# Where the spare projection groups stand in the state-space stage: two whole groups per quarter instead of seven portions

## What is computed

```python
def mixer_block(hn, s_gla, s_c, s_n, s_m, s_re, s_im, P, l):
    (gq, gk, gv, gr, ga, mq, mk, mv, mo, mi, mf, su, za, zb, zc) = split_in(hn @ P['w_in'][l])
    ...
    y_c, re_new, im_new = s5_ssm(su.astype(f32), ...)

def s5_ssm(u, h0_re, h0_im, ...):
    ug = u.reshape(B, T, S5_GROUPS, S5_GROUP)
    bu_re = jnp.einsum('btgc,gpc->btgp', ug, bb_re)
    bu_im = jnp.einsum('btgc,gpc->btgp', ug, bb_im)
    ...
    _, _, hr, hi = lax.associative_scan(combine, (a_re, a_im, bu_re, bu_im), axis=1)
    y = (jnp.einsum('btgp,gcp->btgc', hr, c_re) - jnp.einsum('btgp,gcp->btgc', hi, c_im)
         + d.reshape(S5_GROUPS, S5_GROUP) * ug).reshape(B, T, S5_WIDTH)
    y = jax.nn.gelu(y)
    y = y * jax.nn.sigmoid(y @ w_glu)
```

## Time and profile before

| | |
|---|---|
| median of 3 runs | 2631.93 us |
| the profiled execution's own time | 2638.09 us |
| span of its profile | 2636.3 us |
| TensorE busy, share of the span | 2351.4 us, 89% |
| the state-space stage | from 166.60 to 345.70 |

### The profile page before, as it was taken

The page is one execution under the profiler, slowest core; times in us unless marked ns, Lnnn a source line. Parts: engine busy times, 40 slices in busy tenths (PEclk is TensorE's granted clock), DMA queues, the critical chain, the costliest instruction groups (busy, mean ns, idle before and its releaser), DMA issues.

```text
span 2636.3 us, 34651 instructions
## 1 busy us (share of the span) xinstructions
PE 2351.4 (89%) x14712; PEld 2249.5 (85%) x14712; DVE 1149.7 (44%) x1264; ACT 574.7 (22%) x716; POOL 268.0 (10%) x411
## 2 busy tenths in 40 slices
PE   5799977779985579999999999779999999999996
PEld 5699857568975469999999998669999999999995
DVE  4634413432236532122223432134665666666566
ACT  4422222221321122111212211232211111111112
POOL 6898300000000000000000000000000000000000
PEclk9899988878986669999999999989999999999997
DMA  6211113001210002121112124301111111111111
GB/s 226 87 50 49 49 67 104 17 34 34 80 40 5 16 5 77 48 80 48 47 42 104 48 72 161 135 9 48 52 47 49 48 49 41 49 49 48 41 49 68
DMA packets 35928, 156.35 MB, mean 59 GB/s; under 512 B 4176, under 2 KB 4240, under 8 KB 32336
## 3 DMA queue, kind: packets, MB, share of 16 engines
q1 hardware_dynamic: 27504, 100.22, 11.2%
q0 software_dynamic: 6864, 43.84, 4.3%
q10 hardware_dynamic: 1440, 10.49, 1.0%
HBM read 135.68 MB, written 19.02 MB: 59 GB/s over the span
## 4 chain that ended last, share of the span: by engine, by line
PE 81%; DVE 9%; ACT 5%; issue 3%; DMA 1%; POOL 1%; DVEq 0%; ACTq 0%; POOLq 0%
PE ps L249 21%; PE ps L250 21%; PE ps L252 21%; PE ps L1933 1%; DVE ATT L1565 1%; PE ps L989 1%; PE ps L359 1%; PE ps L360 1%; PE ps L362 1%; DVE CC L1228 1%; DMA scratch_yc<-YC 1%; ACT PA L2000 1%; PE ps L1308 1%; DVE GT L387 1%; PE ps L1609 1%
## 5 line engine op out<-in xcount | busy, mean ns | idle before, releaser
L249 PE MATMUL ps<-XH,WH 128*128 128x344 f32 x1608 | 520.7, 326 | 26.9 <-DVE WL L243 20.7
L250 PE MATMUL ps<-XL,WH 128*128 128x344 f32 x1464 | 469.7, 324 | 0.0
L249 PE MATMUL ps<-XN,WH 128*128 128x344 f32 x1248 | 396.6, 321 | 4.3 <-issue 4.1
L243 DVE TENSOR_TENSOR WL<-WRAW,WH 128x1024 fp32r<-128x1024 f32 x175 | 224.5, 1283 | 393.0 <-ACT WH L238 392.0
L250 PE MATMUL ps<-XN,WH 128*128 128x344 f32 x1248 | 394.7, 319 | 0.0
L252 PE MATMUL ps<-XH,WL 128*128 128x344 f32 x1608 | 345.0, 323 | 0.0
L249 PEld LDWEIGHTS ps<-XH,WH 128*128 128x128 f32 x1608 | 308.3, 192 | 30.9 <-issue 27.6
L238 ACT ACTIVATE WH<-WRAW 128x1024 fp32r<-128x1024 f32 x175 | 184.3, 1054 | 561.0 <-PE ps L252 545.0
L250 PEld LDWEIGHTS ps<-XL,WH 128*128 128x128 f32 x1464 | 280.7, 192 | 0.1
L252 PEld LDWEIGHTS ps<-XH,WL 128*128 128x128 f32 x1608 | 273.0, 191 | 0.0
L252 PE MATMUL ps<-XN,WL 128*128 128x344 f32 x1248 | 262.9, 319 | 0.0
(11 more groups left out here) (503 smaller groups left out, 3293.2 us busy)
## 6 DMA issues: line engine op xcount, KB each, us to landing
WRAW<-in_wslabs SPq DMA_DIRECT2D x175, 512.0 KB, 3.3
XIN<-in_xT POOLq DMA_DIRECT2D x1, 4128.0 KB, 18.4
scratch_mqk<-STAGE SPq DMA_DIRECT2D x8, 516.0 KB, 2.6
XR<-in_xT POOLq DMA_DIRECT2D x1, 4128.0 KB, 12.9
out_y<-XR SPq DMA_DIRECT2D x8, 516.0 KB, 3.0
CACHES<-in_ck ACTq DMA_DIRECT2D x4, 1024.0 KB, 14.3
CACHES<-in_cv ACTq DMA_DIRECT2D x4, 1024.0 KB, 11.9
CACHES<-in_ck POOLq DMA_DIRECT2D x3, 1024.0 KB, 15.7
```

Of the source, the lines that this page charges most:

```text
L243: nc.vector.tensor_tensor(WL[:, slot], WRAW[:, slot], WH[:, slot].bitcast(F32), ALU.subtract).then_inc(w_lo, 1)
L249: pe.matmul(out[t], WH[:, slot, w, :], xh(k, t), start=(k == 0), stop=False)
L250: pe.matmul(out[t], WH[:, slot, w, :], xl(k, t), start=False, stop=False)
```

## The change

The table now gives point a eight k-steps and point c eight, and the other five none. The number of k-steps in a quarter (16) and of groups in all (8) stays. Nothing else is edited.

```diff
 FILL = [(f"{q}{p}", k) for q in range(4) for p, k in
-        (("a", 3), ("b", 2), ("c", 2), ("d", 3), ("e", 2), ("f", 2), ("g", 2))]
+        (("a", 8), ("b", 0), ("c", 8), ("d", 0), ("e", 0), ("f", 0), ("g", 0))]
 FILL_AT = {p: i for i, (p, k) in enumerate(FILL)}
```

## The result

The changed kernel takes 2663.96 us (median of 4 runs, 2663.2 to 2665.81), the kernel before, measured beside it, 2632.97. The ratio is 1.0118, with a 95% interval from 1.0101 to 1.0136: slower by 31.0 us. I had forecast 2661, slower by 29.

The account below looks back on a forecast made before the run. TensorE alone was taken to set the state-space stretch, busy 172.22 of 179.10 us. Stretch +22.3, tail -3.9 and clock +10.6 summed to +29.0 on the median of 2631.93: 2661 us, range 2648 to 2678.

Parts of the forecast that it names:

- Opened waits at b, f and g: TensorE's losses ahead of line 929, after the portion at 203.32, and ahead of line 975: 3.34, 1.5, 0.45 us per quarter.
- At e: TensorE's wait ahead of line 954 for HST, held up by VectorE's split: a loss of 2.0 us per quarter.
- GpSimd quiet at HST: While VectorE's split, product and HST run, GpSimd is idle in all four quarters; otherwise 1.6 us more per such quarter.
- The stretch without the clock, +22.3: State-space stretch: opened waits of 29.2 us less 6.9 us of closed waits, +22.3 us.
- What does not change: Whole kernel: 64 k-steps with the same matmuls, copies, splits, stores and slab loads; only which waits have work changes.
- The clock, +10.6: TensorE in the state-space stretch: eight spells at 0.50 clock, 1.3 us each, +10.6 us; bounds 0 and 21.
- The price of 1.3: TensorE's loss in us for one 3.4 us spell at 0.50, where 14 matmuls fitted instead of 23.
- one spell for each wait: TensorE's clock falls once after each of the eight new waits of 3.34 and 2.0 us.
- The tail, -3.9: Last transpose to line 989: line 896 and the loads 2.9 us earlier, no slab load beside them 1.0, together -3.9.
- its bound of 1.5: Tail: the most that a slab load no longer beside the loads could give, 1.5 us; 1.0 was taken.
- the clock holds: Rival for the state-space stretch: TensorE's clock does not fall, +18.4 us, 2650 us; chance 0.12.
- Faster: Rival: seams close and opened waits total under 10.8 us, clock holding; 8.7 us gained, 2623 us; chance 0.02.

## Why the prediction was right

The total was right (+29 forecast, +31.0 by the medians, +29.9 in stage and tail) and so was the mechanism: the portions were cover, and the opened waits brought the clock down. But three of its terms were off: by -4.9 (the stretch), +4.6 (the clock) and +1.2 (the tail). That they made up for each other, and the total came so close, is luck.

- **Opened waits at b, f and g**, 3.34, 1.5 and 0.45: measured 3.34, 1.42 and 0.44. The rule "from the start of the portion that goes to the moment at which the next line may start" held. **At e**, 2.0: measured 1.74; the split was the last thing that HST waited for, as said, but without it only 0.65 of the wait went away.
- **GpSimd quiet at HST**, four times: right, 1.23 in all four quarters. In quarters 0 and 1 GpSimd itself waited for HST (25.8 us in two waits), and before HST of quarters 2 and 3 it had finished its tables. The run with two k-steps at b showed the other case, and that its price can lie anywhere between quiet and blocked.
- **The stretch without the clock, +22.3**: this step failed in size; with the clock held it is +17.4. Smaller waits give 1.1 to 1.4 of the difference. Most of the rest is a term that I did not have: 28 portions became 8, and borders cost. The portions of the changed kernel sum to 91.8 us for 64 k-steps, those of before to 95.8 without the waits that I had counted. Of these 4.0 us, 1.0 are the seams (0.25 each) and 3.0 the 20 borders, some 0.15 each; 26 and 12 portions without a seam, in two of the other kernels, sum to 93.8 and 92.7, which is 0.1 and 0.2 a portion. (These sums go from the first k-step of a portion to what follows it.) "What does not change" was wrong in this: the same matmuls do not take the same time when they stand in fewer pieces.
- **The clock, +10.6**: this step failed in size too; it is +15.2. The number of spells, eight, was right for this execution, though other kernels here show that one of the four behind e may stay out. The price of 1.3 was read from dense matmuls of 344 columns, and from a spell of 3.4; two were of 6.8, and behind b they lay on lines 929 and 930. They made these lines longer by 2.9 + 1.6 + 2.9 + 1.6 = 9.0 us; the other 6.2 are the four spells at e, so that even a spell of 3.4 cost 1.5 to 1.6. What the prediction took as given, one spell for each wait, held in the changed kernel and is no rule: see the waits of 1.5 at b.
- **The tail, -3.9**: -2.7. The loads gained 1.0, as priced: from the issue of MKV to line 989 it is 9.45 instead of 10.45. No row had shown that price, nor its bound of 1.5; the kernels with and without a slab load beside the loads show it now. Line 896, however, came only 1.7 earlier and not 2.9: without portions at f and g, line 890 is still at work when line 975 ends. Two experiments showed that the split is only the first of three things that line 989 waits for, with the store of the last STAGE and line 890.
- Of the rivals, "the clock holds" did not happen by itself; with the clock held by the extra matmuls, its sum is 14.7 us instead of 18.4. "Faster" never came near: its 10.8 us stand against 27.8 of opened waits (3.34, 1.74, 1.42 and 0.44 in each quarter).

## What to carry to other kernels

What filling work is worth depends on where it stands and not on its amount: price each point by its own wait, and give it just as many pieces as outlast that wait. Let a group end where other work of at least the copy's length follows. Here a table cut by these two rules, with the last group also ended early enough to clear the tail, gained 13.7 us where the whole groups lost 31. When a clock can fall, hold it in one experiment by work that nobody reads: it separates what the waits cost themselves from what they cause.

## What the runs showed of the hardware

- Nearly half of what the opened waits did to the time came through the clock: 17.4 us by waiting, 15.2 by matmuls at the lower level.
- Waits of 1.5 us were followed by a spell at 1.2 GHz in thirteen of fifteen cases at e (four, three, three and three in four kernels) and in none of four at b. Waits of 0.85 at e drew one in one of four, and a wait of 2.0 to 2.2 between dense matmuls in eight of ten profiles.
- A VectorE split that met a GpSimd operation took longer by what was left of that operation, less 0.15 us: 0.32, 0.94 and 1.79 for 0.48, 1.09 and 1.94.
- Changing between these 344-column matmuls of rounded operands and the others costs TensorE some 0.1 to 0.2 us per portion.
